# Attention probabilities transposed in 32 by 32 blocks by VectorE and sent through DRAM, instead of by TensorE

## The reference

```python
# layer 0: local attention with a relative bias; layer 1: "forgetting" attention (decay, causal)
q, k, v, g = split(rms_norm(x) @ w_in)               # per head 256 x 128
sc = q @ k.T * scale + bias_or_decay                  # 256 x 256, the mask included
p  = softmax(sc, axis=-1)
o  = p @ v
x  = x + (o * silu(g)) @ w_out
```

## Time and profile before

| | |
|---|---|
| median of 3 runs | 2439.96 us |
| the profiled execution's own time | 2439.27 us |
| its span | 2437.5 us |
| PE busy | 2408.9 us, 99% |
| DVE busy | 1759.7 us, 72% |
| ACT busy | 1223.9 us, 50% |
| POOL busy | 307.3 us, 13% |
| granted TensorE clock, mean | 0.999 of full |
| DMA | 443.31 MB, 182 GB/s over the span |
| of it from GpSimd's queue | 10.56 MB |

### The profile page before, as it was taken

The page is one execution under the profiler, slowest core; times in us unless marked ns, Lnnn a source line. Parts: engine busy times, 40 slices in busy tenths (PEclk is TensorE's granted clock), DMA queues, the critical chain, the costliest instruction groups (busy, mean ns, idle before and its releaser), DMA issues.

```text
span 2437.5 us, 40472 instructions
## 1 busy us (share of the span) xinstructions
PE 2408.9 (99%) x16588; PEld 2151.4 (88%) x16588; DVE 1759.7 (72%) x2629; ACT 1223.9 (50%) x1811; POOL 307.3 (13%) x401
## 2 busy tenths in 40 slices
PE   7999999999999999999999999999999999999998
PEld 7999999888888888888888888888888888888887
DVE  8998797896767676757666669767576757676766
ACT  6555433675544454445444556554454445444545
POOL 1222114432100000000000001200011001000101
PEclk9999999999999999999999999999999999999999
DMA  8666773386666666675766666767676767767764
GB/s 221 176 160 176 199 184 91 104 223 193 189 187 181 193 182 188 189 188 174 188 196 182 193 169 192 195 180 190 195 187 191 185 190 182 195 187 196 186 176 121
DMA packets 758344, 443.31 MB, mean 182 GB/s; under 512 B 28784, under 2 KB 721136, under 8 KB 758160
## 3 DMA queue, kind: packets, MB, share of 16 engines
q1 hardware_dynamic: 752880, 430.16, 63.9%
q0 software_dynamic: 5280, 10.56, 2.9%
HBM read 437.35 MB, written 3.31 MB: 181 GB/s over the span
## 4 chain that ended last, share of the span: by engine, by line
PE 81%; DVE 3%; issue 1%; ACT 0%; DVEq 0%; ACTq 0%
PE bank L295 40%; PE bank L299 20%; PE bank L325 5%; PE bank L326 5%; PE bank L329 5%; PE bank L1886 1%; PE bank L1901 1%; PE bank L1891 1%; PE bank L1885 1%; PE bank L1902 1%; DVE splitb L260 0%; PE bank L275 0%; PE bank L277 0%; PE bank L276 0%; DVE splita L260 0%
## 5 line engine op out<-in xcount | busy, mean ns | idle before, releaser
L295 PE MATMUL bank<-xx,splitb 128*128 128x512 f32 x3328 | 1154.8, 394 | 1.5 <-DVE mix L2183 0.8
L260 DVE TENSOR_TENSOR splitb<-rawb,splitb 128x1024 fp32r<-128x1024 f32 x672 | 837.3, 1255 | 379.4 <-ACT splitb L254 372.0
L254 ACT ACTIVATE splitb<-rawb 128x1024 fp32r<-128x1024 f32 x672 | 702.1, 1055 | 477.9 <-PE bank L299 325.4
L299 PE MATMUL bank<-xx,splitb 128*128 128x256 f32 x3328 | 920.6, 277 | 0.0
L295 PEld LDWEIGHTS bank<-xx,splitb 128*128 128x128 f32 x3328 | 625.0, 188 | 132.5 <-DVE mix L2183 1.1
L299 PEld LDWEIGHTS bank<-xx,splitb 128*128 128x128 f32 x3328 | 625.0, 188 | 2.4
L295 PE MATMUL bank<-oo,splitb 128*128 128x512 f32 x1008 | 343.3, 389 | 0.0
L275 PE MATMUL bank<-xhl,splita 128*128 128x258 f32 (+1 forms) x1040 | 297.7, 286 | 11.8 <-DVE splita L260 10.6
L277 PE MATMUL bank<-xhl,splita 128*128 128x258 f32 (+1 forms) x1040 | 292.9, 282 | 0.0
L276 PE MATMUL bank<-xhl,splita 128*128 128x258 f32 (+1 forms) x1040 | 292.6, 281 | 0.0
L299 PE MATMUL bank<-oo,splitb 128*128 128x256 f32 x1008 | 278.3, 276 | 0.0
(11 more groups left out here) (298 smaller groups left out, 2255.3 us busy)
## 6 DMA issues: line engine op xcount, KB each, us to landing
rawb<-in_a_w_in_dram SPq DMA_DIRECT2D x256, 512.0 KB, 4.8
rawa<-in_w_in_dram SPq DMA_DIRECT2D x130, 512.0 KB, 5.3
rawb<-in_kv_w_dram SPq DMA_DIRECT2D x128, 512.0 KB, 4.8
rawb<-in_b_w_in_dram SPq DMA_DIRECT2D x128, 512.0 KB, 5.4
rawb<-in_a_w_out_dram SPq DMA_DIRECT2D x64, 512.0 KB, 5.2
rawb<-in_b_w_out_dram SPq DMA_DIRECT2D x64, 512.0 KB, 5.2
rawb<-in_w_out_dram SPq DMA_DIRECT2D x32, 512.0 KB, 5.2
table<-in_rel_dram POOLq DMA_DIRECT2D x32, 128.0 KB, 4.8
```

What stands on the lines that cost most here:

```text
L254: nc.scalar.activation(self.parts(at, h)[0], self.raw_half(at, h), ACT.Copy).then_inc(hi_ready, 1)
L260: nc.vector.tensor_tensor(lo, self.raw_half(at, h), hi.bitcast(F32), ALU.subtract).then_inc(lo_ready, 1)
L295: nc.tensor.matmul(out, hi[:, w], both(k).rearrange("p a t -> p (a t)"), start=start and k == 0, stop=False)
L299: last = nc.tensor.matmul(out[:, 0:SEQ], lo[:, w], both(k)[:, 0], start=False, stop=stop and k == 7)
```

## The change

VectorE transposes each of the 32 by 32 blocks of a head's probabilities in one instruction and writes them into `sc`, free by then. GpSimd stores `sc` to a DRAM scratch (196,608 bytes), waits for that, and issues four loads (one for each 32 partitions of the destination, 49,152 bytes each, in runs of 384 bytes) into one of two buffers `pT`. TensorE no longer transposes, ScalarE no longer copies, and `weigh` waits for the loads and reads `pT` with runs of 32 elements 96 apart. GpSimd's order becomes: table of head 0; then for each `j` the table of head `j` + 1, then the store and loads of head `j`. VectorE's `maxima` of a head waits until the store of the head before has landed, since it writes `sc`.

```diff
+    pr_d = nc.dram_tensor("pr_scratch", [2, 4, 32, 4, 96], F32, kind="Internal").ap()
-    sc, pr, pT = (sbuf(ph, n, [P, W3]) for n in ("sc", "pr", "pT"))
+    sc, pr = (sbuf(ph, n, [P, W3]) for n in ("sc", "pr"))
+    pT = [sbuf(ph, f"pT{b}", [P, W3]) for b in range(2)]
+    NQ, QB = 4, 32
...
+                def turn_probs(g, j):
+                    n = head_no(layer, g, j)
+                    via = pr_d[n % 2]
+                    pool.wait_ge(tr_ready, n + 1)
+                    if n > 1:
+                        pool.wait_ge(pt_in, 16 * NQ * (n - 1))
+                    pool.dma_start(via.rearrange("b r j e -> (b r) (j e)"), sc[:]).then_inc(pr_stored, 16)
+                    pool.wait_ge(pr_stored, 16 * (n + 1))
+                    wait(pool, o_sum, n - 1)
+                    for b in range(NQ):
+                        pool.dma_start(pT[n % 2][QB * b:QB * b + QB, :].rearrange("r (b e) -> r b e", b=NQ),
+                                       via[:, :, b].rearrange("b r e -> r b e")).then_inc(pt_in, 16)
...
                 def heads(g):
+                    head(g, 0)
                     for j in range(GH):
-                        head(g, j)
+                        if j < GH - 1:
+                            head(g, j + 1)
+                        turn_probs(g, j)
...
-                    def turn_probs(j):
-                        pe.wait_ge(p_ready, head_no(layer, g, j) * 2 + 2)
-                        for m in range(3):
-                            last = nc.tensor.transpose(PT[:, P * m:P * m + P], pr[:, P * m:P * m + P], ident[:])
-                        last.then_inc(tr_ready, 1)
...
-                        pe.wait_ge(pt_taken, head_no(layer, g, j) + 1)
+                        pe.wait_ge(pt_in, 16 * NQ * (head_no(layer, g, j) + 1))
...
+                        probs = pT[j % 2][:].rearrange("p (b m c) -> p m b c", b=NQ, m=3)
+                        out = OUTS[j % 2][:, 0:SEQ].rearrange("p (m b c) -> p m b c", m=2, b=NQ)
+                        nc.tensor.matmul(out, vtm[:, 0, w], probs[:, 0:2], start=True, stop=False)
+                        nc.tensor.matmul(out[:, 1], vtm[:, 1, w], probs[:, 2], start=False, stop=True).then_inc(o_sum, 1)
...
                             if j >= 2:
                                 weigh(j - 2)
-                            if 1 <= j <= GH:
-                                turn_probs(j - 1)
...
-                    def take_probs(j):
-                        act.wait_ge(tr_ready, head_no(layer, g, j) + 1)
-                        a(pT[:], PT[:, 0:W3], ACT.Copy).then_inc(pt_taken, 1)
...
                         dve.wait_ge(sc_sum, n + 1)
+                        wait(dve, pr_stored, 16 * n)
...
                             ts(pr[:, parts[m]], pr[:, parts[m]], stat[:, 4 + m:5 + m], None, ALU.mult).then_inc(p_ready, 1)
+                        dve.wait_ge(p_ready, head_no(layer, g, j) * 2 + 2)
+                        v_.transpose(sc[:].rearrange("p (b m c) -> p b m c", b=NQ, m=3),
+                                     pr[:].rearrange("p (m b c) -> p b m c", m=3, b=NQ)).then_inc(tr_ready, 1)
```

More of the change, by code:

```diff
@@ L1487, in _build @@
         sem("sc_sum"), sem("sc_taken"), sem("max_ready"), sem("exp_ready"), sem("p_ready"))
-    tr_ready, pt_taken, v_taken, o_sum, gate_ready = (
-        sem("tr_ready"), sem("pt_taken"), sem("v_taken"), sem("o_sum"), sem("gate_ready"))
+    tr_ready, pr_stored, pt_in, v_taken, o_sum, gate_ready = (
+        sem("tr_ready"), sem("pr_stored"), sem("pt_in"), sem("v_taken"), sem("o_sum"), sem("gate_ready"))
     inv_col, inv_turned = sem("inv_col"), sem("inv_turned")
@@ L1541, in _build @@
     f_ones = sbuf(ph, "f_ones", [AH, SEQ])
-    SC, PT, OT, FZ = psum[2:6]
+    SC, _, OT, FZ = psum[2:6]
     OUTS = [OT, FZ]
@@ L1900, in weigh @@
                         w = slice(j % VB * P, (j % VB + 1) * P)
-                        nc.tensor.matmul(OUTS[j % 2][:, 0:SEQ], vtm[:, 0, w], pT[:, 0:SEQ], start=True, stop=False)
-                        nc.tensor.matmul(OUTS[j % 2][:, P:SEQ], vtm[:, 1, w], pT[:, SEQ:W3], start=False,
-                                         stop=True).then_inc(o_sum, 1)
+                        probs = pT[j % 2][:].rearrange("p (b m c) -> p m b c", b=NQ, m=3)
+                        out = OUTS[j % 2][:, 0:SEQ].rearrange("p (m b c) -> p m b c", m=2, b=NQ)
+                        nc.tensor.matmul(out, vtm[:, 0, w], probs[:, 0:2], start=True, stop=False)
+                        nc.tensor.matmul(out[:, 1], vtm[:, 1, w], probs[:, 2], start=False, stop=True).then_inc(o_sum, 1)
                     def attend(j):
@@ L2079, in heads @@
                             split(q)
-                            if j == 2:
-                                take_probs(0)
                             if 1 <= j <= LAG:
@@ L2089, in heads @@
                             ahead(split_hi, at, 0)
-                            if j <= GH:
-                                take_probs(j - 1)
                             ahead(split_hi, at, 1)
@@ L2220, in second_norms @@
                 dve.wait_ge(f_part, 1)
+                dve.wait_ge(pr_stored, 16 * AH)
                 tt(f_parts, FP, inv, ALU.mult).then_inc(f_scaled, 1)
@@ L2354, in _ @@
                 dve.wait_ge(norm_root, 4 + q)
+                dve.wait_ge(pr_stored, 16 * 2 * AH)
                 v_.reciprocal(invc[:, q:q + 1], invc[:, q:q + 1]).then_inc(norm_inv, 1)
```

## The result

| | before | changed |
|---|---|---|
| median | 2440.07 us (6 runs, 2438.97 to 2440.93) | 2454.95 us (6 runs, 2450.09 to 2460.13) |
| ratio to before | 1 | 1.0062, 95% interval 1.0046 to 1.0077 |
| profiled execution, its span | 2437.5 us | 2451.7 us |

The forecast was 2428 us, the range 2418 to 2446, and the direction was wrong. The runs also spread five times as far as before.

A forecast was written before the change was run, and what follows sets the result against it. The prediction took TensorE, busy 99% of the span, as the bound. It summed 2439.3 - 21 (transpositions removed) + 8 (head 7's waits) + 2 (starts of groups) = 2428 us, range 2418 to 2446.

The forecast's parts named there:

- The bound: TensorE, busy 99% of the span, is never late in the touched stretch: time removed is gained, waits given are added.
- The gain: TensorE loses the three transpositions of each head, 0.32 us a head over 64 heads: -21 us.
- The strided read: weigh reads runs of 32 floats on TensorE: taken as nothing, +38 us if it halved the rate.
- VectorE's transposition: One pass over 384 columns on VectorE: 0.53 us, 0.65 with the wait on its own last result; bounds 0.35 and 1.0.
- Head 7: At weigh of a group's last head, TensorE waits 1.0 us for the loads, eight times: +8 us, at most +49.
- rival A: Head 7's small loads land in 1.7 to 2.4 us on idle engines, no wait: 2418 to 2421 us; chance 0.26.
- Starts of groups: In layer 1, maxima waits 2.3 to 3.8 us for the previous store; TensorE loses 0 to 1.5 in four groups: +2.
- 2.9 us of cover: At layer 1's group starts, VectorE's first tight low part ends 2.9 us before it is needed, absorbing some of its wait.
- the low parts: VectorE work queued behind maxima; the first tight one ends at about 2032.6 and is needed at 2035.48.
- B: At head 7's weigh, transfers cost what they do under load: 4.55 us late, 36 us in all, 2456 us; chance 0.15.
- C: Only head 7's loads are slow: 1.95 to 2.9 us late, 16 to 23 us, so no difference, 2436 to 2443; chance 0.14.

The follow-up runs named there:

- both repairs: Changed kernel with the store issued ahead of the wait for the next tables, and weigh of head 7 placed 2.7 us later: 2419.55 us, ratio 0.9914.
- The second experiment: Changed kernel, sc still shared, with the store of a head put before GpSimd's wait for the next head's tables: 2429.53 us, ratio 0.9954.

## Why the prediction was wrong, point by point

- **The bound**, TensorE with nothing to spare: right. With both repairs the time fell by 21 of the 22.9 us.
- **The gain**, 21 us: 22.9 in clean stretches. The three transpositions cost 0.29 to 0.33 us a head; heads 0 to 3 gave 1.34, and the 0.36 in it is TensorE's pace, which the sum had no term for.
- **The strided read**: nothing, as taken. The step at rounds 8 and 9 is 0.92 us in both (1212.36 - 1211.44 and 1218.48 - 1217.56):

```profile
1211.44 0.39 PE L295 MATMUL bank<-xx,splitb 128*128 128x512 f32 x1
...
1212.36 0.48 PE L295 MATMUL bank<-xx,splitb 128*128 128x512 f32 x1
...
1217.56 0.39 PE L295 MATMUL bank<-xx,splitb 128*128 128x512 f32 x1
...
1218.48 0.48 PE L295 MATMUL bank<-xx,splitb 128*128 128x512 f32 x1
```

- **VectorE's transposition**: 0.58 us against 0.53 for the pass, and 0.61 with the wait before it (2021.94 - 2021.33) against 0.65; all 384 columns in one instruction:

```profile
L2280 DVE STREAM_TRANSPOSE sc<-pr 128x384 f32<-128x384 f32 x64 | 37.0, 579 | 2.2
```

- **Head 7**: right in kind, and in the sum of the waits by an average. Store issued at +5.03 (forecast +5.05), landing in 2.2 to 2.9 us (2.2), last load issued at +9.1 to +9.8 (9.15) and landed at +11.3 to +14.6 (12.35). Waits 8.5 us in sum (8), but from 0.8 to 3.1 in five groups and none in three, not 1.0 in eight. The first three loads took some 2.1 us each, one of them 3.3, as rival A had it; the fourth took 2.1 in three groups and 3.1 to 4.8 in the five where it met the weights, 3.2 on average, as forecast. Two half-clock stretches came on top, so that the five ends lost 12.9 us. By its fit the Trainium skill (DMA: Bandwidth & Descriptors, Anatomy of one DMA) gives 2.45 and 2.1 us for store and load, estimates from the page. The trace agrees for the stores of head 7 (2.2 in most) and for the loads that met no weights (2.1), and disagrees for the loads of all heads (median 4.6).
- **The step that failed: "Starts of groups ... I take 2 us in all".** It was 19.3 us. The mechanism was named, but three things in it were too small. The lateness adds up from head to head: the store of head 0 is itself late and its loads push head 1's tables, so that the store of head 1 left 12.1 to 13.9 us after the scores in layer 1, not 10.4. It then took 4.2 to 6.8 us, not 3.3 to 4.8, and `maxima` of head 2 was 3.0 to 7.5 us late, not 2.3 to 3.8. And I treated 2.9 us of cover as something that swallows most of a wait; what goes beyond it went to TensorE at nearly full price. The way was another too: I had expected it through the low parts, on which TensorE waited 0.8 us; at these starts it waited 9.1 us until VectorE had taken the sums of a gate or q unit, which now stand behind the late `maxima`, the shares and the transposition. For layer 0 I had nothing, and it was 1.6. The second experiment removed the whole term by moving one instruction.
- **A term that was missing: the clock.** Each of TensorE's longer waits was priced at its own length. Five of them had a stretch of 3.4 us at half clock beside them, which costs 1.6 us or a little more: some 8 us of the 14 by which the time rose.
- **The rivals.** B gave 2456, which is the time that came, but by another mechanism: it put 36 us into head 7's wait, which was 8.5 (12.9 with all that those ends lost), so that it hit the time is luck. C, also of late loads, has the same fault. The rival that was needed, "the starts of groups lose 20 us", I had worked out the parts of and not priced at its high end.

## What to carry to other kernels

When a step goes from engines to an in-order queue of transfers, price the queue where the spacing of the work is shortest, and follow it for several rounds: a store that waits behind the next round's load is late by that load, and passes its lateness on. Issue what others wait for first, and wait for what is needed later afterwards; here that one move turned 0.6% slower into 0.5% faster, and with the reader moved 2.7 us back into 0.9% faster. In this kernel, which is bound by TensorE, 12 of the 17 waits over 2 us in the attention layers of all traces had half clock beside them, which cost 1.6 to 2.8 us on top of the wait where it was measured.

## What of the hardware was not expected

- A half-clock stretch of 3.4 us (6.8 with the two waits of 4.65) at waits of about 2 us and more; the granted clock was 1.00 from 600 to 2430 us before. The last 6 to 9 us of the span are at half clock in every trace here, before the change too.
- At full granted clock the same pair of products steps by 0.340 or by 0.353 us, for up to 139 steps on end: 1.7 us at one layer change.
- GpSimd's stores of 192 KB landed in 2.2 us with the DMA engines idle (eight stores of head 7: 2.2 to 2.9), and in up to 6.8 us while weights were in flight.
- With nothing ahead of them, loads of 48 KB landed 2.1 us after their issue; the fourth of head 7, met by the weights, took up to 4.8.
